# Prompt attention on one Trainium2 core: scores by pairs of heads on 64-row halves, ahead of the even head's turn, with four score tiles

## The reference

```
sc = einsum('bcqhd,bckhd->bchqk', chunked(q), k_band) * (d ** -0.5)
sc = where(valid, sc + bias, -inf)          # group A; group B masks what was not selected
p  = softmax(sc, axis=-1)
o  = einsum('bchqk,bckhd->bcqhd', p, v_band)
...
yp = yp + concatenate([o_a, o_b], axis=-1) @ w_out[l]
```

## Time and profile before

| | |
|---|---|
| time before, median of 3 runs | 2840.66 us (2838.58 to 2840.94) |
| the profiled execution: time, span | 2838.89 us, 2837.1 us |
| mean granted TensorE clock, as a share of 2.4 GHz | 0.967 |
| PE busy over the span | 2599.5 us (92%) |
| prompt attention in the span | from 1311 to 1668 us |
| DVE / ACT busy in that stretch | 242.81 us / 209.70 us of 357 us |

### The profile page before, as it was taken

One profiled execution on the slowest core, in us unless ns is written; L12 is line 12 of the kernel. 1 busy time (PEld: TensorE's weight loads), 2 busy tenths in 40 slices (PEclk: granted clock), 3 DMA queues, 4 the chain that ended last, 5 costly groups with the idle time before them and its releaser, 6 DMA issues. The chain is left out here.

```text
span 2837.1 us, 39977 instructions
## 1 busy us (share of the span) xinstructions
PE 2599.5 (92%) x16468; PEld 2322.3 (82%) x16468; DVE 1368.5 (48%) x2391; ACT 993.4 (35%) x1691; POOL 606.9 (21%) x448
## 2 busy tenths in 40 slices
PE   3899999999998999976988989989589999999997
PEld 2899999978878799975776766658489999998886
DVE  6333323244554598985767723332723233234544
ACT  5333333334332313133666532221433333323432
POOL 6333334300001022831000000000344433320000
PEclk9999999999999999987999989999799999999999
DMA  3112222266632121213000334551022121226553
GB/s 104 47 62 79 69 87 79 68 235 219 214 137 67 47 95 64 81 49 121 23 30 24 119 106 151 180 195 52 32 75 79 62 79 62 93 85 243 202 206 126
DMA packets 153108, 294.27 MB, mean 104 GB/s; under 512 B 14032, under 2 KB 90456, under 8 KB 152928
## 3 DMA queue, kind: packets, MB, share of 16 engines
q1 hardware_dynamic: 146688, 268.12, 27.9%
q0 software_dynamic: 6240, 23.59, 2.3%
HBM read 237.26 MB, written 61.78 MB: 105 GB/s over the span
## 5 line engine op out<-in xcount | busy, mean ns | idle before, releaser
L786 DVE TENSOR_TENSOR f_dl<-f_raw_d,f_dh 128x2048 fp32r<-128x2048 f32 x66 | 151.3, 2293 | 274.8 <-ACT f_dh L573 274.8
L573 ACT ACTIVATE f_dh<-f_raw_d 128x2048 fp32r<-128x2048 f32 x66 | 126.5, 1916 | 322.4 <-PE f_pV L151 292.1
L149 PE MATMUL f_pX<-f_xop,f_g_shi 128*128 128x256 f32 (+1 forms) x528 | 159.8, 303 | 18.8 <-ACT f_gh L523 18.8
L523 ACT ACTIVATE f_gh<-f_pX 128x256 f32<-128x256 f32 (+1 forms) x132 | 54.2, 410 | 335.7 <-PE f_pX L151 335.6
L2062 PEld LDWEIGHTS t_po<-t_v,t_pT 128*128 128x128 f32 x1056 | 135.1, 194 | 34.0 <-DVE t_osb L1786 14.3
L149 PE MATMUL f_pX<-f_xop,f_u_shi 128*128 128x256 f32 (+1 forms) x528 | 157.2, 298 | 4.4 <-ACT f_tu L523 4.4
L150 PE MATMUL f_pX<-f_xop,f_g_shi 128*128 128x256 f32 (+1 forms) x528 | 158.7, 301 | 0.0
L151 PE MATMUL f_pX<-f_xop,f_g_slo 128*128 128x256 f32 (+1 forms) x528 | 158.7, 300 | 0.0
L1919 ACT ACTIVATE t_sc<-t_sc,t_small 128x640 f32<-128x640 f32 (+8 forms) x136 | 100.0, 735 | 164.0 <-DVE t_small L1847 129.8
L150 PE MATMUL f_pX<-f_xop,f_u_shi 128*128 128x256 f32 (+1 forms) x528 | 156.8, 297 | 0.0
L151 PE MATMUL f_pX<-f_xop,f_u_slo 128*128 128x256 f32 (+1 forms) x528 | 156.8, 297 | 0.0
(11 more groups left out here) (333 smaller groups left out, 8100.0 us busy)
## 6 DMA issues: line engine op xcount, KB each, us to landing
f_raw_d<-in_ffn_w_down SPq DMA_DIRECT2D x66, 1024.0 KB, 4.9
hid<-f_gh SPq DMA_DIRECT2D x22, 1152.0 KB, 8.6
f_raw_h<-hid SPq DMA_DIRECT2D x66, 384.0 KB, 5.5
f_g_raw<-in_ffn_w_gate SPq DMA_DIRECT2D x22, 1024.0 KB, 5.4
f_u_raw<-in_ffn_w_up SPq DMA_DIRECT2D x22, 1024.0 KB, 6.4
proj<-w_stage POOLq DMA_DIRECT2D x12, 1152.0 KB, 5.6
i_raw<-in_w_in SPq DMA_DIRECT2D x12, 1024.0 KB, 5.2
f_x<-in_x_prompt SPq DMA_DIRECT2D x16, 512.0 KB, 6.4
```

The source lines that it names most:

```text
L149: pe.matmul(out, a[0], b[0], start=first, stop=False, skip_group_check=goes_on)
L523: act.activation(dst, by_tile(pX[:, c, 0:N[c]]), ACT.Copy).then_inc(s_copy, 1)
L573: act.activation(d_hi[slot(q)][:], raw_d[slot(q)][:], ACT.Copy).then_inc(s_dhi, 1)
L786: dve.tensor_tensor(d_lo[slot(q)][:], raw_d[slot(q)][:], d_hi[slot(q)][:].bitcast(F32), ALU.subtract)
```

## The change

For every even head g the list now has `score g+2` and `score g+3` ahead of `turn g`; before, each head's scores followed the turn of two heads earlier. PE issues the two heads' scores together: for each chunk of up to 512 columns first the even head on partitions 0 to 63 into `ps[0]`, then the odd one on partitions 64 to 127 into `ps[1]`. The pair waits until both heads of the pair before it were reduced. `qT` loses its zeros and half its size, ACT fills it with one copy of 128 partitions where there were two of 64, POOL's zeroing goes, and the score ring has four tiles.

```diff
@@ attn_plan
+        if g % 2 == 0 and g + 2 < len(heads):
+            plan += [("score", g + 2), ("score", g + 3)]
         plan.append(("turn", g))
-        if g + 2 < len(heads):
-            plan.append(("score", g + 2))
         if g >= 1:
             plan.append(("value", g - 1))
@@ attn_phase
-        sc = keep("sc", [P, 3, D], F32)
+        sc = keep("sc", [P, 4, D], F32)
-        qT = keep("qT", [P, 2, H, P], F32)
+        qT = keep("qT", [P, 2, HT, P], F32)
-            return sc[:, g % 3, a:b]
+            return sc[:, g % 4, a:b]
@@ gpsimd
-            pool.memset(qT[:], 0.0).then_inc(s_zero, 1)
@@ vector
-                    if g >= 3:
-                        dve.wait_ge(s_t, units[g - 3][-1][0] + 1)
                     if g >= 4:
+                        dve.wait_ge(s_t, units[g - 4][-1][0] + 1)
                         dve.wait_ge(s_p, g - 3)
@@ scalar
-            act.wait_ge(s_zero, 1)
-                    for r in range(2):
-                        i = act.activation(qT[r * HD:(r + 1) * HD, n % 2, r::2, :],
-                                           pm[r * HD:(r + 1) * HD, :].rearrange("p (f c) -> p f c", c=P), ACT.Copy, scale=HD ** -0.5)
-                    i.then_inc(s_ma, 1)
+                    act.activation(qT[:, n % 2, :, :], pm[:].rearrange("p (f c) -> p f c", c=P), ACT.Copy, scale=HD ** -0.5).then_inc(s_ma, 1)
@@ tensor
-                elif e[0] == "score":
+                elif e[0] == "score" and e[1] % 2 == 0:
...
                     if g >= 2:
-                        pe.wait_ge(s_mx, g - 1)
+                        pe.wait_ge(s_mx, g)
                     for c in range(0, nb, 4):
                         c1 = min(c + 4, nb)
-                        last = pe.matmul(ps[g % 2][:, c * P:c1 * P], qT[:, (x * NP + t) % 2, h, :],
-                                         kT[x][:, h // 2, (k0 + c) * P:(k0 + c1) * P], start=True, stop=True)
-                    last.then_inc(s_s, 1)
+                        for r in range(2):
+                            rs = slice(r * HD, (r + 1) * HD)
+                            last = pe.matmul(ps[r][:, c * P:c1 * P], qT[rs, (x * NP + t) % 2, h // 2, :],
+                                             kT[x][rs, h // 2, (k0 + c) * P:(k0 + c1) * P], start=True, stop=True)
+                            if c1 == nb:
+                                last.then_inc(s_s, 1)
```

More of the change, by code:

```diff
@@ L1764, in _ @@
                 else:
-                    pool.wait_ge(s_zero, 3)
+                    pool.wait_ge(s_zero, 2)
                 bv = bd[s % 2][:].rearrange("p (f c) -> p f c", c=5 * DEC_S * 2)
@@ L1883, in _ @@
                     if x == 0:
-                        dve.wait_ge(s_t, (units[NH - 3 + s][-1][0] if s < 3 else punits[s - 3][-1]) + 1)
+                        dve.wait_ge(s_t, (units[NH - 4 + s][-1][0] if s < 4 else punits[s - 4][-1]) + 1)
                         dve.tensor_tensor_reduce(out=in_halves(sc_of(g, 0, KS)), in0=both_halves(g), in1=in_halves(bias_s[:]), scale=1.0, scalar=GONE,
@@ L1975, in _ @@
                     if x == 1:
-                        act.wait_ge(s_t, punits[s - 3][-1] + 1)
+                        act.wait_ge(s_t, punits[s - 4][-1] + 1)
                     act_exp(act, g, KS, sc_of(g, 0, KS) if x == 0 else both_halves(g), sums[:, 0, s % H:s % H + 1])
```

## The result

The changed kernel takes **3050.43 us** (median of 4 runs, 3045.71 to 3058.44) beside 2840.8 us for the kernel before on the same chip: a ratio of **1.0737**, interval 1.071 to 1.0765. The forecast was 2990 us with a range up to 3045. The direction and the waits came as predicted; the time lies 60 us above the number and 5 us above the range.

What follows compares the result with a forecast made beforehand. PE was taken to set the pace before the change, a once-per-pair ring through ACT's order after it. 2838.9 + 110 (ring) + 40 (clock) = 2989, stated as 2990 us; range 2940 to 3045.

Steps and rivals of the forecast that it cites:

- the ring: Prompt attention, once per pair: scores, both reductions, two exponentials, copy, turn and values in series; 420 us in place of 286.
- PE's gaps are ended by the `t_pT` copies: Sign in the trace: PE idle 2 to 3.5 us once per pair, 60 to 120 times, 100 to 170 us in all.
- The pair period: Time from one pair's start to the next at full clock: 9.4 us at 8 blocks, 10.3 at 7, 8.0 at 5.
- the +110: Prompt attention at full clock: 471 us against 357, +114, taken as +110 after ACT's single copy for `qT`.
- bounds 0, 34 and 57 us of PE time: Paired score matmuls: PE saves 0 without overlap, 34 us if starts stay in order, 57 us with full overlap.
- none of it enters the ring: Paired scores: with overlap the even head lands 0.215 us a block after the start, the odd at most 0.43 us later.
- a rival, 0.86 us in each of 32 pairs, +27: Halves don't overlap: from five blocks the even head lands 0.86 us later in 32 pairs, +27 us, 3017; chance 0.12.
- A round trip into 64-row work: Entering and leaving 64-row score matmuls on PE: 0.3 us both ways, 0.2 of it on the ring, 13 us.
- one drop for two pairs and three quarters of it on the ring: PE's gaps in the attention lower the clock: 1.7 us of full-speed work lost per drop, +40 us over 64 pairs.
- The sign that the prediction gave for it: Attention stage in the later trace: near 505 us with the clock loss, granted clock about 0.85 to 0.9.
- the clock falls in nearly every pair: Rival, attention pairs: most of the ring's 134 us of PE work doubles at half clock, +90, 3041 or more; chance 0.07.
- The faster rival: Attention: overlap saves 34 to 57 us less 19 for mode changes, PE still sets the pace, 2803 to 2826; chance 0.04.

Runs made afterwards that it cites:

- experiment 1: Changed kernel with ACT alone back on the list order from before the change, PE and DVE on the new one: 2888.26 us, ratio 1.0168.
- experiment 6: Changed kernel with ACT and DVE both on the old list order, PE still issuing score pairs on halves: 2845.25 us, ratio 1.0012.
- experiment 5: Changed kernel plus two filler matmuls of 512 columns over 128 partitions behind the values of heads 1, 3 and 5: 2998.29 us, ratio 1.0554.
- experiment 4: Changed kernel plus nine small filler matmuls of 64 columns behind the values of heads 1, 3 and 5: 3052.9 us, ratio 1.0729.
- experiment 9: Changed kernel plus two filler matmuls of 512 columns over 64 partitions behind the values of heads 1, 3 and 5: 3056.12 us, ratio 1.0744.
- experiment 8: Changed kernel with scores over all 128 partitions and nine 64-column filler matmuls behind the values of heads 1, 3 and 5: 3028.03 us, ratio 1.0651.
- experiment 3: Kernel before the change, with halved `qT` and each head's scores on its own 64 partitions, one head at a time, old order: 3005.02 us, ratio 1.0571.
- experiment 2: Changed kernel with its new order kept, but score matmuls over all 128 partitions, mixing the pair's scores: 3059.91 us, ratio 1.0771.
- experiment 7: Changed kernel with ACT and DVE on the old list order and PE's paired scores over all 128 partitions: 2863.02 us, ratio 1.0082.

## Why the prediction was wrong where it was

**What bounds the kernel, and the ring: right.** The slowdown is ACT's walk (experiment 1: 162 of 210 us; with DVE's, experiment 6: 205). PE's gaps are ended by the `t_pT` copies, 105.8 us in 53 waits; the prediction had 100 to 170 us in 60 to 120, so there are somewhat fewer. The pair period is 9.48 us for 9.4, at 8 blocks and full clock. In experiment 5, whose fillers keep full clock over more pairs, it is 9.67 at 7 blocks (scores at 1760.89 and 1770.56) for 10.3, and 7.83 at 5 blocks (1507.62 and 1515.46) for 8.0. No run shows the whole stretch at full clock. The line of experiment 5 gives 477 us, with the filler taken as free. The large tiles alone, where it fits the gap, give a better line: the changed kernel and experiments 4, 5 and 9 lie on it within some 2 us, and it ends at about 290 us at full clock, 77 below the 367.1; the clock lost there is 0.305 x 367.1 = 112 us, so a microsecond lost costs 0.69. If that held in the small tiles too (0.38 x 202.4 = 77 lost), they would lose 53 us, and the stretch would take some 440 at full clock. So the ring is worth between 80 and 120 us, an estimate from those lines, and the +110 lies in it.

**The halves: they overlap fully, and enter the ring.** Of the bounds 0, 34 and 57 us of PE time the last is right at 8 blocks (eight records in 1.92 us). That none of it enters the ring holds for the two cases in which they overlap. Where they don't, from five blocks on the even head lands a chunk later, which the prediction priced as a rival, 0.86 us in each of 32 pairs, +27. Experiment 8 has pairs on full rows at full clock, beside the same pairs on halves in experiment 5: 8.50 us (1526.95 to 1535.46) for 7.83 at 5 blocks, 10.34 (1791.63 to 1801.98) for 9.67 at 7, 10.05 (1801.98 to 1812.03) for 9.25 at 8. That is 0.67 to 0.80 us a pair, 21 to 26 us for 32: the rival was priced about right, and its condition didn't come. A round trip into 64-row work is 0.39 us and not 0.3 (experiment 3): 6 us more over 64 pairs.

**The clock: the step that failed.** The prediction has "one drop for two pairs and three quarters of it on the ring: 64 x 0.5 x 1.7 x 0.75 = +40 us". The factor that failed is the 1.7 us of full-speed work for one drop. The number of drops was right: between the first score and the last scaling the granted clock falls from 1.00 to 0.50 33 times, where the product has 32. But it then stays low for 11.5 us on average, 379 us in all, and one drop takes 5.7 us of full-speed work. Together that is (1 - 0.67) x 569.5 = 188 us, where 64 x 0.5 x 1.7 is 54. The share on the ring is not the error: what the clock cost is 569.5 less the 440 to 477 of above, **+93 to +130 us**, or half to seven tenths of the 188, for three quarters predicted. The 212.5 us are then 80 to 120 from the ring and 93 to 130 from the clock; the two add up by the way they were got, and only the large tiles, 77 of their 141 us by the clock, have a line of several kernels behind them. The sign that the prediction gave for it missed too: it had a stage of 505 us at a clock of 0.85 to 0.9.

The earlier trace rows was read as a drop that is over after 5 us, since the kernel before gave the clock back at once. There full-row work without gaps followed. Here another gap followed, and 64-row scores.

**Two causes lie in that, and I had named one.** The gaps: on full rows, where no matmul of the pairs has 64 rows, the order alone lowers the clock to 0.80 (experiment 2, 37 falls, low for 6.1 us on average), and filling its gaps raises it to 0.89 (experiment 8). The halves make no more falls, but each lasts nearly twice as long (33, 11.5 us): at every order and filler tried, the kernel with 64-row matmuls shows the lower clock. It is 0.69 against 0.98 in the old order, 0.67 against 0.80 in the new one, 0.75 against 0.89 with the small filler, 0.87 against 0.97 with the old walks, and 0.75 against 0.88 for a filler of 64 against 128 partitions. Each of these is one profile, but the mean clocks over the whole span bear them out: no execution of a kernel with more 64-row matmuls reaches the lowest clock of its partner (0.906 to 0.916 against 0.929 to 0.934 in the new order, for one). The scores on full rows in experiments 2, 7 and 8 also have other values in them; experiments 3 and 9 differ from their partners without that. The prediction has no term for the 64-row work, and no rival either. The rival "the clock falls in nearly every pair", at 0.07, was the case to be weighed up: its "3041 or more" is where the time fell. It falls once in two pairs only, but since it stays low so long, 61 of the 63 periods from one pair to the next have a part at the low level.

What stays open is which property of 64-row work does it. The smaller rows and the change of mode around them come together in each of these kernels, and in experiment 3 PE leaves and enters the mode in every head; no run has the one without the other. Why the clock came back by 1510 us in experiment 3, fell again by 1590 and came back by 1720 is seen but not explained. Both low stretches begin in the smallest tiles of a group and end in tiles of five blocks; large tiles kept the full clock once they had it.

**The faster rival** stopped where it was said to: the overlap is there, but PE didn't set the pace. Even with the ring gone (experiment 6 against 7) the halves bring 9.3 us of the stretch and 17.8 us of time, not the 38 that overlap less mode changes promised. None of the nine kernels beats the one before.

## What to carry to other kernels

An engine that walks a shared list in order turns a moved entry into a wait of everything behind it. Before moving a producer's work ahead, write down for the consumer engine which small operation (here a copy of 0.6 us) now stands behind which long chain; and if only one engine wants the new order, give that engine alone the new list. Where a change opens a regular gap on TensorE, or replaces 128-row matmuls by 64-row ones, price the clock over the whole stretch and not by one drop seen elsewhere: here it was worth about as much as the ring. A filler for such a gap paid in the large tiles; in the small ones, where it made the pair longer, it mostly cost time.

## What the runs showed of the hardware that was not expected

- TensorE can be busy and slow. In experiment 3 it is busy for 167.25 of 170 us, with no wait over 0.7 us (PEld up to 1.5), and is granted 0.50. The Trainium skill (TensorE: Matmul & The Clock Gate, What's actually happening) has the low clock as the idle state and the high one as the busy state. By that alone experiment 3 would have run at 2.4 GHz; the run differs, and it decides here.
- A filler over 128 partitions lifts the clock (0.67 to 0.88) and makes the kernel 52 us faster with 96 matmuls more; the same filler over 64 partitions leaves the time as it was, with a gain in the large tiles and a loss in the small ones.
- A round trip between 128-row and 64-row float32 matmuls costs 0.39 us of TensorE at full clock (experiment 3), and two heads' float32 scores on the two halves run side by side in 1.92 us, where one took 1.72.
- The clock falls once in two pairs on full rows and on halves alike (37 and 33 falls), but stays low for 6.1 us on full rows and 11.5 us on halves.
